# Hymba-style decoder layer: the head sums of branch 0 as two products on the whole array, those of branch 1 in four quarters

## What is computed

```python
def _head_rmsnorm(o, g):
    bsz, T, H, Dh = o.shape
    of = o.astype(F32)
    y = of * lax.rsqrt(jnp.mean(of * of, axis=-1, keepdims=True) + EPS)
    return (y.reshape(bsz, T, H * Dh) * g.astype(F32)).astype(o.dtype)

o_a = (_head_rmsnorm(o_a, gla_norm[l]) * jax.nn.silu(c['a_z'])).astype(dt)
o_c = (_head_rmsnorm(o_c, hgrn_norm[l]) * jax.nn.silu(c['c_z'])).astype(dt)
```

## Time and profile before

| | |
|---|---|
| timed runs | 1001.17 us median of 3 (1001.0 to 1002.89) |
| the profiled execution | 1002.16 us, its span 1000.4 us |
| mean granted TensorE clock | 0.987 of full speed |
| TensorE busy | 956.1 us, 96% of the span |
| VectorE, ScalarE, GpSimd busy | 62%, 44%, 36% |
| DMA | 56.04 MB, mean 56 GB/s |

### The profile page before, as it was taken

One profiled execution on the slowest core, in us unless ns is written; L12 is line 12 of the kernel. 1 busy time (PEld: TensorE's weight loads), 2 busy tenths in 40 slices (PEclk: granted clock), 3 DMA queues, 4 the chain that ended last, 5 costly groups with the idle time before them and its releaser, 6 DMA issues.

```text
span 1000.4 us, 24114 instructions
## 1 busy us (share of the span) xinstructions
PE 956.1 (96%) x10300; PEld 707.6 (71%) x10300; DVE 616.3 (62%) x1075; ACT 442.2 (44%) x869; POOL 356.7 (36%) x456
## 2 busy tenths in 40 slices
PE   2999789999999999999999999999999999999997
PEld 2858577865787668865887668865886668856683
DVE  4897677727745487536844587536844587447654
ACT  6875455532534335423543335432643345424323
POOL 1213442065402670075303660075303660067200
PEclk9997799999999999999999999999999999999999
DMA  8830341001130012101140013001130014001101
GB/s 310 295 111 3 109 153 53 23 1 43 34 96 1 2 65 64 43 1 43 34 95 2 1 65 75 32 2 43 53 76 1 7 60 85 2 1 44 65 5 45
DMA packets 41517, 56.04 MB, mean 56 GB/s; under 512 B 27793, under 2 KB 28603, under 8 KB 41403
## 3 DMA queue, kind: packets, MB, share of 16 engines
q1 hardware_dynamic: 41411, 54.51, 17.9%
HBM read 38.44 MB, written 9.86 MB: 48 GB/s over the span
## 4 chain that ended last, share of the span: by engine, by line
PE 71%; DVE 17%; ACT 5%; DMA 2%; issue 2%; POOL 1%; SPq 1%; DVEq 0%; ACTq 0%; POOLq 0%
PE pj L832 36%; PE op L1104 15%; PE pj L851 7%; DVE xres L2019 2%; PE sc L920 2%; DVE w_lo L1997 2%; DVE A L2122 2%; PE sc L1124 1%; PE op L1124 1%; DVE X L2291 1%; DMA xin<-in_x_prompt 1%; DMA wo_hi<-in_w_units 1%; PE m L1017 1%; PE sc L968 1%; PE pj L884 1%
## 5 line engine op out<-in xcount | busy, mean ns | idle before, releaser
L832 PE MATMUL pj<-h,w_hi 128*128 128x256 f16 (+1 forms) x3456 | 385.0, 265 | 1.2 <-DVE X L2312 1.1
L832 PEld LDWEIGHTS pj<-h,w_hi 128*128 128x128 f16 x3456 | 309.0, 99 | 54.2 <-issue 11.5
L832 PE MATMUL pj<-h,w_lo 128*128 128x256 f16 (+1 forms) x1728 | 208.8, 264 | 0.0
L832 PEld LDWEIGHTS pj<-h,w_lo 128*128 128x128 f16 x1728 | 157.9, 98 | 17.5
L2122 DVE COPY_PREDICATED A<-cu,sc 64x384 f32<-64x384 uint8 (+1 forms) x168 | 73.8, 439 | 68.1 <-PE sc L920 65.0
L675 POOL TENSOR_TENSOR G<-B 128x256 f32<-128x256 f32 x17 | 12.1, 713 | 181.3 <-DVE B L2052 167.8
L851 PE MATMUL pj<-w_hi,h 128*128 128x512 f16 (+1 forms) x272 | 64.4, 379 | 1.6 <-DVE K L2061 1.2
L1400 ACT ACTIVATE X<-pj 128x512 f32<-128x512 f32 (+1 forms) x45 | 24.9, 554 | 74.5 <-PE pj L832 59.3
L1104 PE MATMUL op<-wo_hi,m_hi 128*128 128x512 f16 x224 | 53.0, 379 | 0.0
L1104 PE MATMUL op<-wo_hi,m_lo 128*128 128x512 f16 x224 | 52.9, 379 | 0.0
L1104 PE MATMUL op<-wo_lo,m_hi 128*128 128x512 f16 x224 | 52.9, 379 | 0.0
(11 more groups left out here) (334 smaller groups left out, 1655.4 us busy)
## 6 DMA issues: line engine op xcount, KB each, us to landing
xin<-in_x_prompt SPq DMA_DIRECT2D x17, 512.0 KB, 4.5
wo_hi<-in_w_units SPq DMA_DIRECT2D x16, 512.0 KB, 5.5
xres<-in_x_prompt SPq DMA_DIRECT2D x15, 512.0 KB, 3.6
out_y_prompt<-xres SPq DMA_DIRECT2D x14, 512.0 KB, 2.6
wo_lo<-in_w_units SPq DMA_DIRECT2D x12, 512.0 KB, 5.6
xres<-in_w_out SPq DMA_DIRECT2D x8, 256.0 KB, 3.4
gpost<-in_w_out SPq DMA_DIRECT2D x8, 256.0 KB, 4.0
m_hi<-in_state_gla SPq DMA_DIRECT2D x1, 512.0 KB, 8.9
```

The costliest lines, as they stand in the source:

```text
L832: m = pe.matmul(b[:, j * T:(j + 1) * T], w[:, k, col + 128 * j:col + 128 * j + 128], h[:, k, :], start=(n == 0 and k == 0), stop=(n == 2 a ...
```

## The change

In tiles 2 to 7 branch 0 of head_sums takes the form that tiles 0, 1 and 8 have: two products of 128x128 with 256 columns, to M1[:, 0:256] and M1[:, 256:512]. With that, branch 0 waits no longer for `yo`. Branch 1 keeps the four quarters, and drops the wait for `nl` of branch 0. In inv_rms branch 0 takes one logarithm of 128x512 from M1 in place of three from two banks; branch 1 keeps its three. Lines below line 1078 move up by two.

```diff
@@ -1070,14 +1070,12 @@
             pe.wait_ge(*at("sq", i, br + 1))
             pe.wait_ge(*at("st", i, NC * (br + 1)))
             X = x_of(i, "AC"[br])
-            if not crossed(i):
+            if br == 0 or not crossed(i):
                 for j in range(2):
                     m = pe.matmul(M1[:, j * TT:j * TT + T], bones, X[:, j, 0:T], start=True, stop=True)
                 m.then_inc(sem("ns", i), 1)
                 return
             pe.wait_ge(*at("yo", i - 1, 2))
-            if br:
-                pe.wait_ge(*at("nl", i, 1))
             for j in range(2):
                 for hh in range(2):
                     out = half(sums_of(j), hh ^ j)
@@ -1613,7 +1611,7 @@
             T, NC, C = dims(i)
             act.wait_ge(*at("ns", i, br + 1))
             X = x_of(i, "AC"[br])[:, :, 0:T]
-            if crossed(i):
+            if br and crossed(i):
                 act.activation(X[:, 0, :], sums_of(0), ACT.Ln, scale=1.0 / HK, bias=cst[:, 0:1])
                 act.activation(half(X, 0)[:, 1, :], half(sums_of(1), 1), ACT.Ln, scale=1.0 / HK, bias=half(cst, 0)[:, 0:1])
                 act.activation(half(X, 1)[:, 1, :], half(sums_of(1), 0), ACT.Ln, scale=1.0 / HK, bias=half(cst, 1)[:, 0:1]
```

## The result

The changed kernel takes 1004.12 us (median of 22 runs, 1002.62 to 1008.26), the kernel before 1001.67 us in as many runs (1000.64 to 1006.0). The ratio is 1.0022, with a 95% interval of 1.0012 to 1.0031: slower by about 2.2 us, between 1.2 and 3.1. The profiled execution took 1003.57 us, with a span of 1001.8. One timed execution of the experiment e7, 1121.92 us at a mean granted clock of 0.842, is in another state than all others here and is left out.

A forecast was written before the change was run, and what follows sets the result against it. The prediction took TensorE, busy 956.1 of 1000.4 us, as the bound. Six calls at +0.40 us gave +2.4, all other parts 0, so 1003.6 us on the median 1001.17, range 1001.9 to 1004.3.

The forecast's parts named there:

- The price of the call: Branch 0's head_sums call on TensorE, tiles 2 to 7: 1.56 us against 1.16, 0.40 us more per call.
- the model of tile 8: Tile 8's whole-product call, also waiting for the states: 0.62 us to the first product, 0.94 from it to the next projection.
- The lower bound: Branch 0's call priced from tile 1's warm whole products, 0.86 less 0.59: +0.27 us per call, +1.6 in all.
- The upper one: Branch 0's call priced as two more passes at the warm rate: 0.43 us per call, +2.6 us in all.
- The idle time as a wait for the states: TensorE's 0.39 us without columns ahead of branch 0's quarters, labelled "issue", is a wait for VectorE's states.
- Rival B: That idle time is the array changing from whole to quarters: -0.12 us per call, -0.7 in all, 1000.5 us; chance 10%.
- The shift passes through the tile: TensorE's 0.40 us delay shifts gate_in and the chain to conv_out equally, so the 0.2 us conv_out waits stay.
- Rival A: VectorE's chain to conv_out stays put, so TensorE regains that wait in five tiles: +1.3 us, 1002.5 us; chance 22%.
- ScalarE's saving, worth 0: Branch 0's single logarithm saves ScalarE 0.73 us per tile, but this ends in a wait off the path: 0 us.
- The waits that went, worth 0: TensorE's dropped waits for yo (branch 0) and nl (branch 1) are covered by other waits or old signals: 0 us.
- The sum: Six calls at 0.40 us: +2.4 us on the median 1001.17, giving 1003.6 us; chance 62%.

The follow-up runs named there:

- e7: The changed kernel with VectorE's y_out ahead of the states scaling 512 of 1024 columns in tiles 2 to 7: 1002.35 us, ratio 0.9997 to the kernel before.
- e2: The kernel before, quarters kept, with VectorE's y_out ahead of the states scaling 512 of 1024 columns in tiles 2 to 7: 1000.07 us, ratio 0.9975.
- e3: The changed kernel with branch 1 also as two whole products and one logarithm: 1005.23 us, ratio 1.0032 to the kernel before.
- e5: The kernel before with the four quarter products of branch 0 issued twice in tiles 2 to 7: 1004.47 us, ratio 1.0028.
- e10: The changed kernel with the dropped waits back, yo ahead of branch 0's call and nl ahead of branch 1's: 1003.9 us, ratio 1.0018 to the kernel before.
- e1: The changed kernel with three logarithms again for branch 0 in tiles 2 to 7 in place of one: 1004.93 us, ratio 1.0033 to the kernel before.
- e8: The kernel before, quarters kept, with y_out cut in halves by bank, one ahead of the states, one behind: 1008.95 us, ratio 1.0072.

## Why the prediction was right

**The price of the call.** 0.40 us from the model of tile 8, 0.39 measured. The lower bound (+0.27) took the warm row of whole products and so missed 0.07 us of their passing behind a wait and 0.04 of their start. The upper one (+0.43) gave the quarters no price: e2, e3, e5 and e7 show that they pay 0.10 us on the way in and 0.16 out, and e10 that the wait hides the first. That the forecast came so near is the merit of the row it was taken from. Tile 8's call has the same products and the same wait, and it has, like the changed call, two waits and not three. The prediction didn't name that likeness.

**The idle time as a wait for the states.** Shown by e2 (no wait once VectorE is early) and by the changed kernel's own label. Rival B had 10%, and is excluded. The label "issue" goes with the number of waits: it came back when e10 put the third one back.

**The shift passes through the tile.** The call grew by 0.39, the tile by 0.37 to 0.38. The reading of ScalarE's gate_in holds (timeline of ScalarE, then VectorE, in the changed kernel):

```profile
272.58 0.60 ACT L1398 ACTIVATE X<-pj 128x512 f32<-128x512 f32 x1 [0.66 <-PE pj L832]
```

```profile
273.21 0.69 DVE L2331 SCALAR_TENSOR_TENSOR X<-X 128x512 f32<-128x512 f32 x1 [0.47 <-ACT X L1398]
```

ScalarE now waits 0.66 us for TensorE (0.29), VectorE 0.47 us for ScalarE, where it had waited less than some 0.1; conv_out follows TensorE at the same distance. Rival A is excluded by that, and by the wait for conv_out, 1.2 us in all.

**ScalarE's saving, worth 0.** Shown by e1: the logarithm in one (682 ns in the mean over ten) took 0.7 us off ScalarE and nothing off the tile.

**The waits that went, worth 0.** This part was wrong by a little. Neither wait was the last to end, as the prediction says, but with both put back the call is 0.04 us shorter (e10), so dropping them cost 0.2 us in the six tiles. It did no harm to the sum, since the 0.62 us of tile 8 had that cost in it.

**The sum.** 2.4 us forecast, 2.3 from the calls in the trace, 2.2 by the ratio (1.2 to 3.1), 2.45 between the medians. The time itself, 1004.12 us, is 0.5 above the forecast 1003.6: the forecast stood on a median of three, 1001.17, and 22 runs of the kernel before have 1001.67. The change is close to what can be told from no change, and its interval does not tell on which side of 0.2% it lies; the length of the tile does tell that it is not nothing.

## What to carry to other kernels

Price an operation in the state in which it will run: the same exchange of four quarter products for two whole ones cost 0.17 us behind a projection and 0.35 us behind a wait (0.39 with the wait that was dropped). Measure from the instruction that releases it to the next one of its engine, and look for a call of the wanted form that had the same wait. An idle time labelled "issue" ahead of an instruction with several waits may be a wait for another engine: look for a signal that lands just ahead of it. Before a gap in one tile is taken for the price of an edit, look at the same place in all tiles: the 0.46 us of e8 stood in one of six. And before work is reordered on an engine with 62% busy time, count its slack on the chain that matters: VectorE's was 0.1 us per tile, and e8 paid some ten times that.

## What the runs showed of the hardware

Four 64x64 float32 products on four different quarters took 0.43 us of 256 columns when repeated, exactly half of two 128x128 products (0.87), so they ran fully beside each other; a change from the projection's products on the whole array to the quarters cost 0.10 us and the change back 0.16. I had seen the first and not the second. Two whole products took 0.94 us behind a wait where they take 0.87 in a stream. The same first product started 0.61 to 0.62 us after the start of the instruction it waited for when its call had two waits, and 0.57 when it had three (the changed kernel and e10).
